# Attention by tile units: banded heads with stationary values, part of the gate product between the units

## The reference, cut to what matters

```
h = rms_norm(x);  proj = h @ w_in + b_in  -> qa ka va | qb kb vb | ga gb
branch A: 8 query heads of 64, 2 key/value heads; 128-token blocks, each sees its own
          block and the one before (window 128), with a sink logit per head in the softmax
branch B: 4 heads, each with two causal softmax maps p0, p1 over all keys;
          a = p0 - lam * p1;  o = a @ vb;  o = rms_norm(o per head) * diff_subln_g * 0.8
ya = oA @ w_swa_out;  yb = oB @ w_diff_out
mixed = sigmoid(ga) * ya + sigmoid(gb) * yb;   x = x + mixed @ w_o
x = x + mixture of experts(rms_norm(x))        (top 4 of 32 experts)
out = rms_norm(x)
```

## Time and profile before

| what | value |
| --- | --- |
| median of 3 runs | 3001.46 us (2997.08 to 3006.98) |
| the profiled execution | 3002.64 us |
| its span, first to last instruction | 3000.8 us |
| mean granted TensorE clock | 0.931 of full speed |
| TensorE busy with matmuls | 2642.1 us (88%) |
| VectorE / ScalarE / GpSimd busy | 1481.6 / 364.6 / 724.8 us |
| HBM traffic over the span | 166 GB/s |

### The profile page before, as it was taken

How to read it: one execution, slowest core, us unless ns; L and a number is a source line. 1 busy time by engine, 2 the same in 40 slices (tenths; PEclk the granted TensorE clock), 3 DMA queues, 4 the chain that set the end, 5 groups by cost and what they waited for, 6 DMA issues and landing times.

```text
span 3000.8 us, 63110 instructions
## 1 busy us (share of the span) xinstructions
PE 2642.1 (88%) x22972; PEld 1187.1 (40%) x22973; DVE 1481.6 (49%) x2879; ACT 364.6 (12%) x870; POOL 724.8 (24%) x623
## 2 busy tenths in 40 slices
PE   8999988899998868799999989899889879997755
PEld 4644666444444422244433424234333323332212
DVE  4342787201114445466666656565555546664334
ACT  2001554100001200000000000000000000000002
POOL 0000000000000323244444424244334333442112
PEclk9998798899999879899999989999999999998878
DMA  3100000500025478731556283935786775579993
GB/s 134 56 28 1 1 1 1 154 28 21 21 86 173 143 245 320 255 119 26 191 179 200 71 306 106 363 113 176 258 296 211 242 273 186 189 249 368 378 355 133
DMA packets 166005, 499.22 MB, mean 166 GB/s; under 512 B 46032, under 2 KB 82384, under 8 KB 132944
## 3 DMA queue, kind: packets, MB, share of 16 engines
q1 hardware_dynamic: 108176, 459.96, 40.8%
q0 software_dynamic: 29168, 38.39, 6.7%
q10 hardware_dynamic: 28608, 0.19, 0.5%
HBM read 466.64 MB, written 32.15 MB: 166 GB/s over the span
## 4 chain that ended last, share of the span: by engine, by line
PE 41%; DMA 26%; issue 1%; SPq 1%; DVE 1%; ACT 0%; DVEq 0%; ACTq 0%; POOLq 0%; POOL 0%
PE xbank L1283 24%; DMA w_hi<-in_w 17%; PE xbank L1306 13%; DMA reg_r<-in_w 9%; PE xbank L1251 3%; PE xbank L1293 1%; PE xbank L1300 0%; DVE reg_h L1213 0%; PE xbank L1237 0%; DMA w_hi<-in_b 0%; SPq L868 0%; DMA reg_h<-acc_rows 0%; PE xbank L1224 0%; SPq L877 0%; DMA acc_rows<-stage,idxs 0%
## 5 line engine op out<-in xcount | busy, mean ns | idle before, releaser
L1183 DVE COPY reg_r<-reg_r 128x2048 f32 x580 | 678.5, 1225 | 467.4 <-DMA reg_r<-in_w 219.5
L1283 PE MATMUL xbank<-reg_r,stage 128*32 128x512 f32 x4640 | 572.5, 630 | 102.6 <-DVE reg_r L1183 81.0
L1306 PE MATMUL xbank<-reg_r,stage 128*32 128x256 f32 x9280 | 561.3, 391 | 79.8 <-DMA reg_r<-in_w 79.4
L1283 PE MATMUL xbank<-w_hi,stage 128*32 128x512 f32 x4640 | 555.2, 613 | 58.4 <-DMA w_hi<-in_w 58.3
L1306 PEld LDWEIGHTS xbank<-reg_r,stage 128*32 128x32 f32 x9280 | 312.5, 113 | 318.1 <-DMA reg_r<-in_w 103.4
L933 POOL DMA_INDIRECT acc_rows<-stage,idxs x145 | 340.9, 2351 | 120.9 <-POOL idxs L930 110.0
L1283 PEld LDWEIGHTS xbank<-reg_r,stage 128*32 128x32 f32 x4640 | 157.9, 114 | 427.6 <-issue 277.1
L1283 PEld LDWEIGHTS xbank<-w_hi,stage 128*32 128x32 f32 x4640 | 153.5, 112 | 393.4 <-issue 261.7
L930 POOL TENSOR_TENSOR idxs<-idxa,tok 128x1 int32<-128x1 int32 x145 | 28.8, 199 | 971.1 <-ACT stage L1000 940.0
L531 PE MATMUL pair<-reg_r,reg_h 128*128 128x512 f32 (+1 forms) x640 | 253.2, 551 | 0.3 <-DMA reg_r<-in_w_in 0.3
L923 POOL DMA_INDIRECT stage<-xn_rows,idxg x147 | 192.8, 1311 | 121.5 <-POOL idxg L920 113.0
(11 more groups left out here) (187 smaller groups left out, 1959.8 us busy)
## 6 DMA issues: line engine op xcount, KB each, us to landing
reg_r<-in_w SPq DMA_DIRECT2D x256, 1024.0 KB
w_hi<-in_w SPq DMA_DIRECT2D x128, 1024.0 KB, 5.6
idxa<-slot_rows ACTq DMA_DIRECT2D x596, 0.2 KB
reg_r<-in_w_in SPq DMA_DIRECT2D x4, 2048.0 KB, 7.9
reg_r<-in_x SPq DMA_DIRECT2D x8, 512.0 KB, 3.4
reg_ka<-in_w_in SPq DMA_DIRECT2D x8, 512.0 KB, 3.8
reg_g<-in_w_in SPq DMA_DIRECT2D x8, 512.0 KB, 3.9
reg_r<-in_w_o SPq DMA_DIRECT2D x1, 4096.0 KB, 17.1
```

The source lines that it names most:

```text
L1183: dve.tensor_copy(w1k[k], lo_from[:, bass.ds(slot, 1), k, :].rearrange("p o n -> p (o n)")).then_inc(w1_filled[k], 1)
L1283: ins = pe.matmul(up_bank[b][QB * c:QB * c + QB, :].rearrange("p (h k q) -> p h k q", h=2, q=QB), xT[b][:, QB * k:QB * k + QB], w1k[k].rea ...
L1306: ins = pe.matmul(y_bank[b][QB * j:QB * j + QB, 0:DG], actT[b][:, QB * k:QB * k + QB], w2r[:, k, j * DG:(j + 1) * DG], start=False, stop=( ...
```

## The change

`UNITS` has five units for each block i: one banded unit that holds all eight banded heads, then the four differential ones, 40 in all. In a banded unit the scores of the eight heads are issued in turn between the two row halves, head h of pair[0] and of pair[1]; the probabilities are turned by a true matmul whose moving operand is a diagonal matrix with the reciprocals of the row sums (built by GpSimd, 128 x 512 for four heads), so that they come out turned and scaled; and the values are stationary, 64 columns for each key/value head, with 512 turned columns moving, so that the output comes out transposed and goes straight to qaT. oan and its transposes are gone. The scaling and the squares of the diff outputs (`finish`) move from VectorE to ScalarE; the outputs of branch B are normed by the same diagonal in their turn, with the gain as a scale of one value a partition. `fill` puts 64 of the 256 gate matmuls (branch A, the first four column blocks) at the end of the turns of the attention loop, by the list `FILLS`; ScalarE copies each result to mixT and takes its sigmoid from there later. The four slabs for it are loaded within the loop, as are four more. After the loop the gate products run two steps ahead of the branch products; w_swa_out, w_diff_out and w_o are issued right after the last product; x is loaded in eight tiles with a semaphore each.

```diff
-UNITS = [(kind, i, j) for i in range(NT) for j in range(4) for kind in ("swa", "diff")]
+UNITS = [(kind, i, j) for i in range(NT) for kind, j in [("swa", 0)] + [("diff", j) for j in range(4)]]
+AHEAD = 4
+FILLS = [2] * 15 + [2, 2, 2, 1, 1] * 2 + [2, 2, 1, 1, 1] + [2, 1, 1, 1, 1] + [1, 1, 1, 1, 1]
...
+SLABS = [(d, 0) for d in range(AHEAD)] + [(d, 1) for d in range(AHEAD)] + [(d, br) for d in range(AHEAD, KD) for br in range(2)]
+def gates_of(m):
+    return [1] if m // 2 < AHEAD else [0, 1]
...
+            load_gate(0)
+            load_gate(1)
+            for n in (2, 3):
+                sp.wait_ge(fill_done, 2 * (n - 1))
+                load_gate(n)
+            sp.wait_ge(pv_ready, UNITS.index(("swa", NT - 1, 0)) + 1)
+            load_gate(4)
+            load_gate(5)
...
             sp.wait_ge(pv_ready, NU)
...
-            sp.wait_ge(gate_ready, 4 * KD)
-            sp.dma_start(x2, a["x"][0].rearrange("(t p) n -> p t n", p=P)).then_inc(x_back, 16)
+            sp.wait_ge(gate_ready, gates_before(2 * KD - 1, 1) + 1)
+            for t in range(NT):
+                sp.dma_start(x2[:, t, :], x_d[t]).then_inc(x_back[t], 16)
+        @block.gpsimd
...
+                    pool.wait_ge(r_ready, i + 1)
...
+                    for c in range(2):
+                        pool.tensor_tensor(diag[c], ident.unsqueeze(1).to_broadcast([P, 4, P]),
+                                           r8[:, 4 * c:4 * c + 4].unsqueeze(2).to_broadcast([P, 4, P]), ALU.mult).then_inc(diag_ready, 1)
...
+                        for h in range(4):
+                            at = 4 * c + h
+                            ins = act.activation(probs[u % 2][c][:, h * n:(h + 1) * n], pair[c][:, h * n:(h + 1) * n], ACT.Exp,
+                                                 bias=nm8[:, at:at + 1], scale=ATT_SCALE, accum_out=ls8[:, at:at + 1])
...
+                if kind == "swa":
+                    act.wait_ge(sinks_ready, i + 1)
+                    act.activation(se8, sk8, ACT.Exp).then_inc(exp_ready, 1)
...
+                    for c in range(2):
+                        act.wait_ge(low_turned, low_turns(u) + c + 1)
+                        act.activation(pT_s[c][:, 0:512], bank[4][:, :], ACT.Copy).then_inc(pT_act, 1)
...
+            def finish(u):
+                kind, i, j = UNITS[u]
+                act.wait_ge(pv_ready, u + 1)
+                if kind == "swa":
+                    act.activation(qaT[:, :, i * P:(i + 1) * P], bank[6][:, :].rearrange("p (j q) -> p j q", j=4),
+                                   ACT.Copy).then_inc(o_taken, 1)
+                    return
+                r = rinv[:, 2 * (u % 4):2 * (u % 4) + 1]
+                act.activation(junk_q, bank[6][:, 0:P], ACT.Square, scale=r, accum_out=ssb[:, 4 * i + j:4 * i + j + 1])
+                act.activation(obn[:, i, j, :], bank[6][:, 0:P], ACT.Copy, scale=r).then_inc(o_taken, 1)
...
+                if kind == "swa" and i:
                     for c in range(2):
+                        dve.wait_ge(high_turned, high_turns(u) + c + 1)
+                        dve.tensor_copy(pT_s[c][:, 512:1024], bank[5][:, :]).then_inc(pT_dve, 1)
...
+                if kind == "swa":
...
+                    for h in range(4):
+                        for c in range(2):
+                            ins = pe.matmul(pair[c][:, h * n:(h + 1) * n], qaT[64 * c:64 * c + 64, h, i * P:(i + 1) * P],
+                                            kaT[64 * c:64 * c + 64, k0:k0 + n], start=True, stop=True)
...
+                    for c in range(2):
+                        pe.wait_ge(diag_ready, 2 * i + c + 1)
+                        if c:
+                            pe.wait_ge(pT_act, low_turns(u) + 1)
+                            if i:
+                                pe.wait_ge(pT_dve, high_turns(u) + 1)
+                        for m in range(n):
+                            for h in range(4):
+                                ins = pe.matmul(bank[4 + m][:, h * P:(h + 1) * P],
+                                                probs[u % 2][c][:, (h * n + m) * P:(h * n + m + 1) * P], diag[c][:, h, :],
+                                                start=True, stop=True)
...
+                    for m, kt in enumerate(keys):
+                        for c in range(2):
+                            ins = pe.matmul(bank[6][64 * c:64 * c + 64, :], va[:, kt, c * HD:(c + 1) * HD],
+                                            pT_s[c][:, m * 512:(m + 1) * 512], start=(m == 0), stop=(m == len(keys) - 1))
...
+            def fill(at, n):
+                for x in range(at, at + n):
+                    g, k = divmod(x, KD)
+                    d, half = divmod(g, 2)
+                    slot, use = SLOT_OF[d]
+                    if k == 0:
+                        pe.wait_ge(gw_in[slot], 16 * use)
+                        if g:
+                            pe.wait_ge(fill_taken, g)
+                    ins = pe.matmul(bank[7], ring[slot].rearrange("p (k n) -> p k n", k=KD)[:, k, :],
+                                    hT[:, k, half * 512:(half + 1) * 512], start=(k == 0), stop=(k == KD - 1))
+                    if k == KD - 1:
+                        ins.then_inc(fill_done, 1)
...
                 if 1 <= u <= NU:
                     turn_p(u - 1)
+                if u < NU:
+                    fill(sum(FILLS[:u]), FILLS[u])
+            gates(0)
+            pe.wait_ge(o_taken, NU)
             for i in range(NT):
...
+                pe.wait_ge(scale_ready, i + 1)
...
+                    ins = pe.matmul(bank[4 + i % 2][:, j * P:(j + 1) * P], obn[:, i, j, :], diag[i % 2][:, j, :], start=True, stop=True)
                 ins.then_inc(o_turned, 1)
+            pe.wait_ge(fill_taken, 2 * AHEAD)
+            gates(1)
             pe.wait_ge(wsd_in, 48)
...
             for m in range(2 * KD):
...
+                if m + 2 < 2 * KD:
+                    gates(m + 2)
+                branches(m)
...
             def residual(t):
-                if t == 0:
-                    dve.wait_ge(x_back, 16)
+                dve.wait_ge(x_back[t], 16)
```

More of the change, by code:

```diff
@@ L298, in _, with take_fill @@
+            def take_fill(g):
+                d, half = divmod(g, 2)
+                act.wait_ge(fill_done, g + 1)
+                act.activation(mixT[:, d, half * 512:(half + 1) * 512], bank[7], ACT.Copy).then_inc(fill_taken, 1)
             act.wait_ge(late_in, N_LATE)
-            for u in range(NU + 1):
+            filled = [sum(FILLS[:u]) // KD for u in range(NU + 1)]
+            for u in range(NU + 2):
+                if 1 <= u <= NU and filled[u] > filled[u - 1]:
+                    take_fill(filled[u - 1])
@@ L311, in _ @@
[L311 to L317, removed]
+                act.wait_ge(o_turned, i + 1)
+                act.activation(qbT[:, :, i * P:(i + 1) * P], bank[4 + i % 2].rearrange("p (j q) -> p j q", j=4),
+                               ACT.Copy, scale=sub_c).then_inc(obT_ready, 1)
@@ L419, in maxima @@
                         dve.tensor_scalar(nm[:, s:s + 1], mx[:, s:s + 1], -ATT_SCALE, None, ALU.mult).then_inc(max_ready, 1)
-            def exp_count(u):
-                return 2 * u + 2 * units_before("swa", u)
+                if kind == "swa":
+                    dve.drain()
+                    dve.tensor_tensor(sk8, sinks, nm8, ALU.add).then_inc(sinks_ready, 1)
             def mix(u):
@@ L592, in product @@
                 keys = keys_of(UNITS[u])
[L593 to L605 removed]
+                pe.wait_ge(pT_act, low_turns(u + 1))
@@ new lines, in gates @@
+            def gates(m):
+                d, half = m // 2, m % 2
+                for br in gates_of(m):
+                    slot, use = SLOT_OF[SLABS.index((d, br))]
+                    pe.wait_ge(gw_in[slot], 16 * use)
+                    if m >= 2:
+                        pe.wait_ge(gate_sig, 2 * (m - 2) + br + 1)
+                    for k in range(KD):
+                        ins = pe.matmul(gate_bank(m, br), ring[slot].rearrange("p (k n) -> p k n", k=KD)[:, k, :],
+                                        hT[:, k, half * 512:(half + 1) * 512], start=(k == 0), stop=(k == KD - 1))
+                    ins.then_inc(gate_ready, 1)
@@ new lines, in branches @@
+            def branches(m):
+                d, half = m // 2, m % 2
+                for br in range(2):
+                    if m >= 2:
+                        pe.wait_ge(mix_done, m - 1)
+                    oT = (qaT, qbT)[br]
+                    for j in range(4):
+                        ins = pe.matmul(bank[2 + br + 2 * (m % 2)], w_sd[:, br, j, d * P:(d + 1) * P],
+                                        oT[:, j, half * 512:(half + 1) * 512], start=(j == 0), stop=(j == 3))
+                    ins.then_inc(y_ready, 1)
```

294 lines of the change are left out of this document (140 added, 154 removed).

## The result

The changed kernel takes 2929.24 us (median of four runs, 2922.48 to 2932.03) against 3000.49 for the kernel before: ratio 0.9751, interval 0.9732 to 0.9770. A later set gave 2936.03 against 3002.12, ratio 0.9785 (0.9748 to 0.9822). Its profiled execution took 2927.53 us, with a span of 2925.7.

The account below looks back on a forecast made before the run. PE was taken as the bound, busy 88%, with holes in the attention loop from chains and time lost to a lower clock. 3002.6 - 68 (gates) - 1 (loop) - 3 (second half) = 2930.6, median 2929; range 2912 to 2945.

Parts of the forecast that it names:

- The gate and branch stage: Behind the attention loop: 64 matmuls moved away, oan turns and the w_diff_out wait gone; 355.9 to 288 us, -68.
- Diff units: Attention loop: VectorE and ScalarE chain sets periods of 2.5 to 6.3 us, 144 in all; PE just fits.
- Banded units: Attention loop: eight units, all chain, 11.3 us each for seven and 7 for i = 0, 86 us together.
- the tail: End of the attention loop: mix, turn, copy and product after the last exponential, 6 us.
- The clock's price: Attention loop: PE holes in banded units leave a sixth of the loop at 1.2 GHz, +14 us.
- The diagonal: GpSimd's diagonal product in banded units: 1.3 us, most of it beside the next scores and product.
- Side by side tiles: Attention loop: row halves overlap, eight banded scores take 1.95 us with latency; any tiling-mode drain is within that latency.
- The start of the second half: Wait for the first residual: x arrives before b1 is asked for, between nothing and 6 us saved, -3 taken.
- the clock holding: Rival, 12%: chain shorter and fills keep PE dense; loop 236 us or a little less, total 2914.
- fills hide nothing: Rival, 15%: PE is already the limit at 1.2 GHz, holes move rather than fill; loop 293 us, total 2973.
- the slow diagonal: Rival, 15%: GpSimd takes 4 us for the diagonal, loop +25 to +30 us, total 2957.
- the fallen clock: Rival, 3%: the clock falls, slower than before; at 1.2 GHz throughout the loop, 3109 us.

Follow-up runs that it names:

- the run without cover: Changed kernel with gates(0) and gates(1) moved behind the turning of the diff outputs and the wait for the branch weights: 2952.17 us, ratio 0.9813.
- the aligned fills: Changed kernel with five fills in each banded turn, none in the next, one in each of the other three, in every block: 2909.53 us, ratio 0.9668.
- mix first: Changed kernel with VectorE mixing the first diff unit between the two copies of the banded unit's turned probabilities, not behind both: 2935.71 us, ratio 0.9761.
- the same with the mix first: Changed kernel, five fills in banded turns, none next, one or two after, none at i = 7; first diff mix between banded copies: 2921.92 us, ratio 0.9744.

## Why the prediction came out

**The gate and branch stage** was right: -71.4 us against -68, at the edge of the bounds, 284.6 against 288, and the run without cover shows both covers that I had named: waits of 3.7 and 4.8 us where I had reckoned 4 and 6, and about 5 us of slow clock behind them that I had not counted. I had added 5 us for a slow clock and the last steps; as the fills keep TensorE dense to the end, it was about one.

**Diff units** were right in cause and a little too long. Forecast 2.5, 3.3, 3.8, 4.3, 4.8, 5.3, 5.8, 6.3; without fills ScalarE's rows give 2.4, 3.0, 3.6, 4.1, 4.6, 5.1, 5.6, 6.1, with the slope that I had put (0.51 us a key block). Four heads of each make 138 us and not 144. With the change's fills the last period of a block is the same to 0.25 us. That TensorE fits is true there, and not for the period nearer to the banded unit at i = 0 to 4.

**Banded units** are the step that failed, by its size. I took 86 us for their chain, 14 for the clock and 6 for the tail: 106 in all. The loop of 261.1 less 138 leaves 123. So the miss of 11 us in the loop (261 against 250) is 17 us too little here, less 6 us too much for the diff units. The chain was sized nearly right: the aligned fills measure it at 11.2 to 12.5 where I had 11.3 (at i = 0, 10.8 where I had 7), 8 us too little with the tail. The other part I missed: with two fills behind the second half of the turn TensorE has a backlog there, as they are not in a hole but in front of the next scores. The mix that I had put on the chain is then waited for by nobody (mix first); where no fill stands there it is on the chain, as put (the same with the mix first). And where the fills lie in the hole before the scores, the clock stays up too. How the 23 us between the change and the aligned fills divide between clock and placing no run separates. The four profiles of the same code moved by 7.4 us for 0.03 of clock; by that slope, which is an estimate, the 0.06 from 0.93 to 0.99 would be some 15 us and the placing some 8. The clock's price was right in kind. From 310 to 315 us the granted clock is 0.77 and from 315 to 320 it is 0.50, the lower of its two levels, 1.2 GHz, just behind the banded unit's holes; the turn there takes 3.75 us a half, against 2.02 at full clock:

```profile
310.00:315.00 5.00, 3.29 (x11) 2.25 (x12) 1.81 (x12) 4.03 (x19) 2.04 (x2) 0.77 0.00 0
315.00:320.00 5.00, 4.12 (x20) 3.86 (x19) 0.69 (x1) 0.60 (x1) 0.00 (x0) 0.50 0.00 0
...
```

```profile
313.87 3.75 PE L674 MATMUL bank<-early,reg_r 128*128 128x128 f32 x16
318.50 3.75 PE L674 MATMUL bank<-early,reg_r 128*128 128x128 f32 x16 [0.88 <-DVE early L551]
```

**The diagonal**: 1.04 us against 1.3 taken from the rows. The Trainium skill's figure (GPSIMD Engine Reference, "Performance versus the Vector engine") had given an estimate of 1.1 us; here the trace agrees with it. That it is the wrong engine is true of its speed (VectorE does the same shape in 0.69) and doesn't matter, since in the one run with twice the work TensorE waited 4.6 us for it in all, against 0.9.

**Side by side tiles**: eight scores in 2.00 us as put (1.95). The Trainium skill's rule that a change of tiling mode drains TensorE (TensorEngine Tiling (Array Packing), "Key Properties") shows no gap here either: L703 starts at 366.90 while L642's row ends at 366.97. As a row's end is modelled, a drain as short as that latency can't be seen.

**The start of the second half**: 3 us taken, 0.7 measured. The wrong step is that x delays b1 by 3 us: b1's last part takes 7.1 us to land with x long in, and x had added 0.7.

**Sum.** Stages give -71.4 + 3 to 11 (loop, by its clock) - 0.7 = -61 to -69 us, and the second set's ratio of 0.9785 is -64.5. The first set's -71 and the hit of 2929 to within a microsecond owe some us to the experts' part, which wanders by 20 us between executions. That the loop of the aligned fills came within 2 us of my 236 for a full clock owes something to luck too: diff units too long by 6 us stood against banded units and tail too short by 8. Of the rivals, the clock holding is what the aligned fills reach (237.9 us at 0.99), "fills hide nothing" is refuted by the run without them, and neither the slow diagonal nor the fallen clock came.

## What to carry to other kernels

Filler work for TensorE is free only where its own order waits for another engine. Find those places in its timeline, put the filler directly before the waiting instruction, and not behind a long burst, where it is a delay; and see that the filler's own hand-over (here a bank that ScalarE must copy out) doesn't fall inside the hole, since the engine that makes the hole is the one that is busy. What is on the chain depends on where the filler stands: here VectorE's order was worth nothing with filler behind the turn and 0.5 to 0.7 us a block without. Here filled holes paid twice, because the granted clock stayed at its higher level (0.99 in the loop with aligned fills, 0.93 to 0.96 in the change). Before a stage is called bound by one engine, take the filler away and see whether the period moves.

## What the hardware showed that I had not expected

Four profiles of the same loop differ by 7.4 us (253.7 to 261.1), with the mean clock 0.96 to 0.93; with the holes filled the clock was 0.99 and the loop 16 us below the shortest of them. And the part of the kernel that no edit touched varied from 1913.7 to 1948.1 us over fourteen profiles: for a change worth less than that, only the stages of the trace can say where it went.
